# A layer's windowed attention: one overlaid score square per head in place of two, and a 0/1 band multiplied in after the turn

## The chip, the cores and the metric

One core of one Trainium2 chip runs the whole program. The metric is device time in microseconds of one execution, median of several. The engines named here are TensorE (PE), VectorE (DVE), ScalarE (ACT) and GpSimd (POOL). They run their own instruction streams in order and meet only at semaphores.

## The reference

The program is a first block (short convolution, sparse attention, cross attention, FFN) and then a second block of two layers, on 512 tokens of width 1024. The change is in the second block's attention, which has 16 query heads of width 64, two key/value heads and a window of 128 tokens:

```
def sliding_window_attention(q, k, v, sinks):          # BLOCK = WINDOW_2 = 128
    qb = q.reshape(B, nb, BLOCK, N_KV_HEADS, GROUP, HEAD_DIM)
    kb, vb = band(k), band(v)              # previous block of 128 keys, then the query's own block
    s = einsum('bnqkgd,bnskd->bnkgqs', qb, kb) * HEAD_DIM ** -0.5
    rel = qi + BLOCK - sj                  # qi: 0..127, sj: 0..255
    mask = (rel >= 0) & (rel < WINDOW_2) & (kpos >= 0)
    s = where(mask, s, -inf)
    m = maximum(max(s), sink)
    p = exp(s - m);  p = p / (sum(p) + exp(sink - m))
    o = einsum('bnkgqs,bnskd->bnqkgd', p, vb)
```

With window and block both 128, query r of a block sees key s of its own block where s <= r, and key s of the previous block where s > r. So of the two 128 x 128 squares of a head each position is live in exactly one. Around the attention stand a wide input projection, a 31-tap convolution with a layer norm, gates, an output projection and an FFN.

## The kernel before

Everything is float32. The large products are made of three float32r products each (hi*hi, hi*lo, lo*hi; lines 415 to 417), fed by weight units that DMA brings, ACT splits into hi (line 297) and DVE into lo (line 301, in halves lines 793 and 797). They are nearly all of PE's work.

The attention of a layer is 32 jobs (`LJ`). Job j is one pair of heads (e = 0, 1) and one block of 128 queries; `block_of` takes blocks 1, 2, 3 and last block 0, so jobs 0 to 23 have two squares (previous block and own block) and jobs 24 to 31 only their own. The jobs run through a software pipeline, written out by hand: a loop over steps t, of which each engine has its own version, in the same order of t. Of a job j:

- PE, step j, `scores`: two products of 64 x 256 columns into two PSUM banks (`score_bank`, alternating between two pairs).
- DVE, step j, `softmax`: for each e one fused instruction (line 2415) that scales the scores, adds the mask, writes `lprob` and takes the running minimum of the negated scores, over 256 columns; after these, the reciprocal of the row sums of job j-1 (line 2419).
- ACT, step j, `exps` (line 2260): two exponentials of 257 columns (the 257th is the sink, put there by POOL, `sink_column`), with row sums.
- POOL, step j+1, `scaled` (line 2590): multiplies the 2 x 256 probabilities of a row with the reciprocal.
- PE, step j+3 (`LAG_T`), `turn` (line 2120): four transposes of 128 x 128 into bank 4.
- ACT, step j+3, `copy_turned` (line 2267): bank 4, 512 columns, to `lprobT` (two buffers). It is the first thing ACT does in a step.
- PE, step j+4 (`LAG_V`), `values` (line 2133): four products with the values into bank 6, last thing in a step but for the sums below.
- DVE, step j+4, `gated` (line 2427): bank 6 times the gate into `sga`.

In the jobs of block 0 all of it is half as wide, and `turn` and `values` have two instructions for each four.

Between `turn` and `values` PE does a number of the layer's large products, `FILL_AT`[t]; steps 0, 4, 8, 11 and 13 have none. At the end of step 3 PE sums the convolution's output over channels (`ln_sum`, line 2170), which waits for the last of 124 convolution taps on DVE (line 2345; three taps ahead of the loop, three in step 0, two in step 1). DVE takes the mean (line 2473) and subtracts it (line 2476), ACT squares (line 2289; channels 0, 1 in step 3, 2, 3 in step 4), POOL adds the squares (line 2604; one addition in step 6, two in step 7), and PE sums them at the end of step 7 (line 333).

The tail: from step 29 POOL adds the convolution's half to the attention's half of output tile k = t-29 (`merged`, line 2595), ACT rounds it (`merged_hi`, line 2273, last in ACT's step), DVE takes the remainder (`merged_lo`, line 2440, from step 30), and PE multiplies tile k with the output weights in step 32+k, k = 0 to 3 (`OUT_AT`: nine products in a step); tiles 4 to 7 come after the loop. Tile 7 is added on DVE in the last step, ahead of that step's `merged_lo`.

Of the kernel before, what the change touches and what calls it, by code (L numbers as in the profile page):

```python
# [25 lines left out]
I32 = mybir.dt.int32  # L26
ALU = mybir.AluOpType
# [73 lines left out]
def build(nc, w, x, mem, pos, pack, tables, cmask, w2, wg, rope2, out):  # L101
    ctx = ExitStack()
    with ctx:
# [118 lines left out]
        tab2 = place("tab2", [P, 2 * T + 2 * P], F32, a)  # L222
        cos2, sin2 = tab2[:, 0:T], tab2[:, T:2 * T]
        perm2, heads2 = tab2[:, 2 * T:2 * T + P], tab2[:, 2 * T + P:]
# [6 lines left out]
        lprob = place("lprob", [P, 4, 2, 2 * P + 2], F32, b)  # L231
        lprobT = place("lprobT", [P, 2, 4, P], F32, b)
# [411 lines left out]
        def _(sp):  # L644
# [38 lines left out]
        kc_step, vc_done, kc_rope, kcm_ready, kcm_dup, vblk_ready = (  # L683
            sem(n) for n in ("kc_step", "vc_done", "kc_rope", "kcm_ready", "kcm_dup", "vblk_ready"))
# [115 lines left out]
        def mixer1_pe(pe):  # L800
# [122 lines left out]
            def c_scores(i):  # L923
                if i == 0:
                    pe.wait_ge(kcm_dup, 1)
# [150 lines left out]
        def mixer1_act(act):  # L1076
# [100 lines left out]
            act.wait_ge(kcm_ready, 1)  # L1177
            act.activation(kcm[HD:P, :, :], kcm[0:HD, :, :], ACT.Copy).then_inc(kcm_dup, 1)
# [105 lines left out]
        def mixer1_dve(dve):  # L1284
# [104 lines left out]
            dve.tensor_copy(kcm[0:HD, :, 0:NCMP], kc2[:, :, :]).then_inc(kcm_ready, 1)  # L1389
# [456 lines left out]
        def cross_dve(dve):  # L1846
# [76 lines left out]
            for j in range(11):  # L1923
# [5 lines left out]
        l_u, l_ugs, l_sig, l_a, l_tap, l_q, l_vt, l_v_turned, l_v = (sem("l_" + n) for n in (  # L1929
            "u", "ug_scaled", "sigmoid", "a", "tap", "q", "v_raw", "v_turned", "v"))  # L1930
# [7 lines left out]
        A = {n: sem("a_" + n) for n in ("scores", "max", "exp", "rec", "scaled", "turned", "turned_copied",  # L1938
                                        "pv", "gated")}
# [9 lines left out]
        LAG_T, LAG_V = 3, 4  # L1949
# [16 lines left out]
        MERGE_HI_AT, MERGE_LO_AT = 29, 30  # L1966
        OUT_AT = {32: (0,), 33: (1,), 34: (2,), 35: (3,)}
        STEPS = LJ + LAG_V

        def prob_at(j):  # L1970

            return (0, 1, 3, 2)[j % 4]
# [25 lines left out]
        def layer_pe(pe, L):  # L1998
# [38 lines left out]
            for n in range(3, V_FILL):  # L2037
# [8 lines left out]
                if n == V_KV + 1:  # L2046
                    pe.wait_ge(l_vt, L + 1)
                    for b_ in range(QB):
                        mm = pe.transpose(bank[:, AUX, b_ * P:(b_ + 1) * P], acc[:, b_ * P:(b_ + 1) * P], ident[:, :])
                    mm.then_inc(l_v_turned, 1)  # L2050
# [62 lines left out]
            def turn(j):  # L2113
                first = 1 if block_of(j) == 0 else 0
# [32 lines left out]
            for t in range(STEPS):  # L2147
# [11 lines left out]
                if t in OUT_AT:  # L2159
                    if t == LJ:  # L2160
# [26 lines left out]
        def layer_act(act, L):  # L2187
# [21 lines left out]
            for n in range(V_FILL):  # L2209
# [6 lines left out]
                if n == V_KV:  # L2216
                    act.wait_ge(unit_done, u.n + 1)

                    act.activation(acc[:, :], bank[:, 2 * u.slot + 1, :], ACT.Copy).then_inc(l_vt, 1)
# [17 lines left out]
                if n == V_KV + 1:  # L2237
                    act.wait_ge(l_v_turned, L + 1)
# [15 lines left out]
            def exps(j):  # L2254
                c0 = P if block_of(j) == 0 else 0
                act.wait_ge(sink_in, L * LJ + j + 1)
                for e in range(2):
                    act.wait_ge(A["max"], (L * LJ + j) * 2 + e + 1)
                    row = lprob[:, prob_at(j), e, c0:2 * P + 1]
                    act.activation(row, row, ACT.Exp, bias=asm(j, 0, e), scale=-1.0, accum_out=asm(j, 4, e)).then_inc(A["exp"], 1)  # L2260

            def copy_turned(j):
                act.wait_ge(A["turned"], L * LJ + j + 1)
                if j >= 2:
                    act.wait_ge(A["pv"], L * LJ + j - 1)
                first = 1 if block_of(j) == 0 else 0
                act.activation(lprobT[:, j % 2, :, :].rearrange("p (e c) t -> p e c t", e=2)[:, :, first:, :],
                               bank[:, 4, :].rearrange("p (e c t) -> p e c t", e=2, c=2)[:, :, first:, :], ACT.Copy)\
# [55 lines left out]
        def layer_dve(dve, L):  # L2324
# [76 lines left out]
            def softmax(j, o):  # L2401

                j, o = j if j < LJ else None, o if 0 <= o < LJ else None
                if j is not None:
                    c0 = P if block_of(j) == 0 else 0
                    if j == 0:
                        dve.wait_ge(q_inv, L * 2 + 2)
                    if j in (2, 3):
                        dve.wait_ge(q_rope, L * 9 + j + 6)
                    if j >= 4:  # L2410
                        dve.wait_ge(A["turned"], L * LJ + j - 3)
                    for e in range(2):
                        c = 2 * (j % 8) + e
                        dve.wait_ge(A["scores"], (L * LJ + j) * 2 + e + 1)
                        dve.tensor_tensor_reduce(lprob[:, prob_at(j), e, c0:2 * P], bank[:, score_bank(j) + e, c0:2 * P], mask_b[:, c0:2 * P],  # L2415
                                                 query_factor(j, e), neg_sink[:, L, c:c + 1], ALU.add, ALU.min, asm(j, 0, e)).then_inc(A["max"], 1)
                if o is not None:
                    dve.wait_ge(A["exp"], (L * LJ + o + 1) * 2)
                    dve.reciprocal(asm(o, 12), asm(o, 4)).then_inc(A["rec"], 1)  # L2419

# [127 lines left out]
        def _(pool):  # L2548
# [28 lines left out]
            def sink_column(L, j):  # L2577
                if j in (2, 3):
                    pool.wait_ge(q_rope, L * 9 + j + 6)
# [3 lines left out]
                pool.tensor_copy(lprob[:, prob_at(j), :, 2 * P], sinks).then_inc(sink_in, 1)  # L2583

            def scaled(L, j):
                c0 = P if block_of(j) == 0 else 0
# [172 lines left out]
```

## Time and profile before

| | |
|---|---|
| time, median of 3 runs | 2248.24 us (2246.92 to 2248.31) |
| span of the profiled execution | 2246.4 us (the page gives no other time for it) |
| busy in it | PE 2224.9, PE weight loads 1821.7, DVE 1245.1, ACT 885.6, POOL 280.7 us |
| chain that ended last | PE 93%, DVE 3%, POOL 1%, ACT 1%, issue 1% |
| granted PE clock | 0.999 mean |
| the loop over the steps in the two layers | 1033 to about 1155 and 1725 to about 1847 us from the span's start |

Times in a timeline are microseconds from the span's start. PE's instructions overlap: the time that one costs is the distance from its start to the next one's start, not its duration. A duration on DVE, ACT and POOL also overlaps the next one of that engine by some tens of nanoseconds. A bracket at a line's end is the engine's idle time ahead of it and what ended it.

### The profile page before, as it was taken

What the parts mean: (1) busy time and instruction counts of PE and PEld (TensorE: products, weight loads), DVE (VectorE), ACT (ScalarE), POOL (GpSimd) and SP (SyncE); (2) the same over time, 40 slices, a digit from 0 to 9 for tenths busy, and PEclk for the clock granted to TensorE, in tenths of its full rate; (3) what the DMA queues carried; (4) which work ended last, traced back from release to release, by engine and by line L of the source; (5) the groups of instructions that cost most, each with busy time, mean ns of one, the idle gap of its engine ahead of it and who ended that gap; (6) DMA issues with size and microseconds to landing.
All of it is one profiled execution on the core that took longest, in us unless ns stands there. A gap on an engine that the chain in (4) does not pass through costs nothing.

```text
span 2246.4 us, 29245 instructions
## 1 busy us (share of the span) xinstructions
PE 2224.9 (99%) x11388; PEld 1821.7 (81%) x11388; DVE 1245.1 (55%) x1836; ACT 885.6 (39%) x1363; POOL 280.7 (12%) x273
## 2 busy tenths in 40 slices
PE   9999999999999999999999999999999999999999
PEld 7877888898888888886778888888887668888887
DVE  6467656445444225999664444333889664544422
ACT  5545454354333225234744333222323753433321
POOL 3000032011000001014331000001003442000000
PEclk9999999999999999999999999999999999999999
DMA  6221033122222231321122222222221112322222
GB/s 223 100 76 57 20 121 126 55 72 99 103 102 93 94 113 69 113 75 57 56 77 81 107 93 93 100 106 105 104 84 57 39 66 85 113 102 104 94 101 86
DMA packets 30484, 203.19 MB, mean 90 GB/s; under 512 B 3504, under 2 KB 4144, under 8 KB 6704
## 3 DMA queue, kind: packets, MB, share of 16 engines
q1 hardware_dynamic: 29088, 197.34, 24.4%
q10 hardware_dynamic: 1296, 4.46, 0.5%
q8 instruction: 69, 1.13, 0.2%
q14 instruction: 31, 0.25, 0.0%
HBM read 199.69 MB, written 2.10 MB: 90 GB/s over the span
## 4 chain that ended last, share of the span: by engine, by line
PE 93%; DVE 3%; POOL 1%; ACT 1%; issue 1%; DMA 0%; ACTq 0%; DVEq 0%; POOLq 0%
PE bank L415 26%; PE bank L417 26%; PE bank L416 26%; PE bank L2110 1%; PE bank L1002 1%; PE bank L2120 1%; PE bank L2133 1%; PE bank L973 1%; PE bank L2028 1%; POOL acc L324 1%; PE bank L990 1%; PE bank L2010 1%; PE bank L1593 1%; PE bank L1570 1%; PE bank L515 1%
## 5 line engine op out<-in xcount | busy, mean ns | idle before, releaser
L415 PE MATMUL bank<-x_hi,w_hi 128*128 128x512 f32 (+1 forms) x2032 | 789.9, 389 | 5.9 <-DVE x_lo L1766 2.3
L417 PE MATMUL bank<-x_hi,w_lo 128*128 128x512 f32 (+1 forms) x2032 | 775.0, 381 | 0.0
L416 PE MATMUL bank<-x_lo,w_hi 128*128 128x512 f32 (+1 forms) x2032 | 774.1, 381 | 0.0
L301 DVE TENSOR_TENSOR w_lo<-w_raw,w_hi 128x2048 fp32r<-128x2048 f32 x167 | 386.2, 2313 | 412.3 <-ACT w_hi L297 412.3
L297 ACT ACTIVATE w_hi<-w_raw 128x2048 fp32r<-128x2048 f32 x167 | 319.7, 1916 | 585.8 <-PE bank L417 583.9
L415 PEld LDWEIGHTS bank<-x_hi,w_hi 128*128 128x128 f32 x2032 | 382.1, 188 | 83.6 <-issue 6.8
L417 PEld LDWEIGHTS bank<-x_hi,w_lo 128*128 128x128 f32 x2032 | 381.9, 188 | 74.9
L416 PEld LDWEIGHTS bank<-x_lo,w_hi 128*128 128x128 f32 x2032 | 382.4, 188 | 72.7 <-issue 2.9
L415 PE MATMUL bank<-f_hi,w_hi 128*128 128x512 f32 (+1 forms) x572 | 213.3, 373 | 0.0
L416 PE MATMUL bank<-f_lo,w_hi 128*128 128x512 f32 (+1 forms) x572 | 213.2, 373 | 0.0
L417 PE MATMUL bank<-f_hi,w_lo 128*128 128x512 f32 (+1 forms) x572 | 213.2, 373 | 0.0
L2345 DVE SCALAR_TENSOR_TENSOR cy<-la,gains,cy 128x512 f32<-128x512 f32 x240 | 173.9, 794 | 0.0
L563 DVE TENSOR_TENSOR bank<-bank,rbc 128x512 f32<-128x512 f32 x66 | 46.0, 697 | 167.6 <-PE bank L417 159.6
L415 PEld LDWEIGHTS bank<-f_hi,w_hi 128*128 128x128 f32 x572 | 107.7, 188 | 19.0
L416 PEld LDWEIGHTS bank<-f_lo,w_hi 128*128 128x128 f32 x572 | 107.7, 188 | 18.9
L417 PEld LDWEIGHTS bank<-f_hi,w_lo 128*128 128x128 f32 x572 | 107.7, 188 | 18.7
L324 POOL TENSOR_TENSOR acc<-acc,sq 128x512 f32<-128x512 f32 (+1 forms) x48 | 77.6, 1618 | 144.2 <-ACT sq L308 140.4
L552 ACT ACTIVATE f_hi<-bank 128x512 f32 x66 | 39.6, 599 | 115.5 <-DVE bank L569 115.5
L571 DVE TENSOR_TENSOR f_lo<-bank,f_hi 128x512 f32 x66 | 45.7, 692 | 58.4 <-ACT f_hi L552 58.4
L2590 POOL TENSOR_TENSOR lprob<-lprob,small 128x512 f32<-128x512 f32 (+1 forms) x64 | 61.9, 967 | 123.6 <-DVE small L2419 77.8
L2260 ACT ACTIVATE lprob<-lprob,small 128x257 f32<-128x257 f32 (+1 forms) x128 | 60.5, 475 | 31.5 <-DVE small L2415 30.9
L324 POOL TENSOR_TENSOR acc<-sq 128x512 f32<-128x512 f32 (+1 forms) x8 | 14.4, 1801 | 442.8 <-ACT sq L308 442.8
(355 smaller groups left out, 2637.2 us busy)
## 6 DMA issues: line engine op xcount, KB each, us to landing
w_raw<-w_d SPq DMA_DIRECT2D x184, 1024.0 KB, 4.8
out_d<-h SPq DMA_DIRECT2D x8, 256.0 KB, 6.6
h<-x_d ACTq DMA_DIRECT2D x3, 512.0 KB, 9.2
tab<-rope_d ACTq DMA_DIRECT2D x2, 640.0 KB, 3.9
memT<-mem_d ACTq DMA_DIRECT2D x1, 1024.0 KB, 4.8
w_raw<-w_d SPq DMA_DIRECT2D x2, 256.0 KB, 4.1
h<-x_d ACTq DMA_DIRECT2D x2, 256.0 KB, 5.8
w_raw<-w_d SPq DMA_DIRECT2D x1, 512.0 KB, 6.6
```

Source lines behind the costliest of these rows:

```text
L297: act.activation(w_hi[:, u.slot, :], w_raw[:, u.slot, :], ACT.Copy).then_inc(hi_ready, 1)
L301: dve.tensor_tensor(w_lo[:, u.slot, :], w_raw[:, u.slot, :], w_hi[:, u.slot, :], ALU.subtract).then_inc(lo_ready, 1)
L324: pool.tensor_tensor(acc[:, 0:width], sq[:, 0, 0:width] if k == 1 else acc[:, 0:width], sq[:, k % 2, 0:width], ALU.add).then_inc(acc_ready, 1)
L415: pe.matmul(dst, wh[:, k, cols], hi[:, kx_, at:at + width], start=start, stop=False)
L416: pe.matmul(dst, wh[:, k, cols], lo[:, kx_, at:at + width], start=False, stop=False)
L417: return pe.matmul(dst, wl[:, k, cols], hi[:, kx_, at:at + width], start=False, stop=stop)
L552: act.activation(pick(f_hi, j, i), up, ACT.Copy).then_inc(f_hi_done, 1)
L563: dve.tensor_tensor(g, g, rbc[:, :], ALU.mult).then_inc(gu_scaled, 1)
L571: dve.tensor_tensor(pick(f_lo, j, i), up, pick(f_hi, j, i), ALU.subtract).then_inc(f_lo_done, 1)
L2260: act.activation(row, row, ACT.Exp, bias=asm(j, 0, e), scale=-1.0, accum_out=asm(j, 4, e)).then_inc(A["exp"], 1)
L2345: dve.scalar_tensor_tensor(out=cy[:, m, :], in0=src, scalar=wt, in1=cy[:, m, :], op0=ALU.mult, op1=ALU.add).then_inc(l_tap, 1)
L2590: pool.tensor_tensor(row, row, asm(j, 12).unsqueeze(2).to_broadcast([P, 2, 2 * P - c0]), ALU.mult).then_inc(A["scaled"], 1)
```

## The change

- Jobs 0 to 23: DVE first copies, with one predicated copy for both heads, the previous block's square over the own block's square wherever s > r. The own square then holds the 128 live scores of a row. The predicate is the own square's mask (bf16, read as 16-bit integers; nonzero where s > r). `max`, `exp`, `scaled` and `turn` then handle one square per head: 128 columns, and two transposes per job.
- DVE's order in a step is now predicated copy(t), reciprocal(t-1), then the two fused instructions of t. The copy waits for both heads' scores, the fused instructions for the copy.
- `copy_turned` moves 256 columns, and waits for POOL's `banded` of two jobs before.
- New on POOL: `banded`, in step j+3 after `scaled`: one multiplication of 512 columns (256 in block 0) that makes from the turned square two squares, times the 0/1 bands r > s and r <= s. It waits for `copy_turned`(j) and for `values`(j-2). The result `lband` goes to `values`, whose four products stay.
- `LAG_V` is 5, `STEPS` 37. `merged`, `merged_hi`, `merged_lo` and the output products all start one step later (30, 30, 31, 33). `FILL_AT` and the other tables stay, so step 32 has no large product.
- The table read by DMA per layer grows by 256 columns. `lprob`, `lprobT` are smaller and start elsewhere, so waits on the rope move from jobs 2, 3 to job 0. Some semaphores are joined.

```
@@ LAG_T, LAG_V = 3, 4      ->  LAG_T, LAG_V = 3, 5
@@ MERGE_HI_AT, MERGE_LO_AT = 29, 30  ->  30, 31
@@ OUT_AT = {32: (0,), 33: (1,), 34: (2,), 35: (3,)}  ->  {33: (0,), 34: (1,), 35: (2,), 36: (3,)}
 turn(j):
-                for e in range(2):
-                    for c in range(first, 2):
-                        mm = pe.transpose(bank[:, 4, (2 * e + c) * P:(2 * e + c + 1) * P], lprob[:, prob_at(j), e, c * P:(c + 1) * P], ident[:, :])
+                for e in range(2):
+                    mm = pe.transpose(bank[:, 4, e * P:(e + 1) * P], lprob[:, prob_at(j), e, 0:P], ident[:, :])
 values(j):
-                pe.wait_ge(A["turned_copied"], L * LJ + j + 1)
+                pe.wait_ge(A["banded"], L * LJ + j + 1)
...
-                                       lprobT[:, j % 2, 2 * e + c, :], start=(c == first), stop=(c == 1))
+                                       lband[:, j % 2, c, e, :], start=(c == first), stop=(c == 1))
 copy_turned(j):
                 if j >= 2:
-                    act.wait_ge(A["pv"], L * LJ + j - 1)
+                    act.wait_ge(A["banded"], L * LJ + j - 1)
...
+                act.activation(lprobT[:, j % 2, :, :].rearrange("p e t -> p (e t)"), bank[:, 4, 0:2 * P], ACT.Copy)\
 softmax(j, o):
+                first = j is not None and block_of(j) == 0
+                if j is not None and not first:
+                    pair = bank[:, score_bank(j):score_bank(j) + 2, :]
+                    dve.wait_ge(A["scores"], (L * LJ + j + 1) * 2)
+                    dve.copy_predicated(pair[:, :, P:2 * P], mask_b[:, P:2 * P].bitcast(U16).unsqueeze(1).to_broadcast([P, 2, P]),
+                                        pair[:, :, 0:P]).then_inc(A["packed"], 1)
                 if o is not None:
                     dve.wait_ge(A["exp"], (L * LJ + o + 1) * 2)
                     dve.reciprocal(asm(o, 12), asm(o, 4)).then_inc(A["rec"], 1)
+                if j is not None:
...
+                    if not first:
+                        dve.wait_ge(A["packed"], L * 24 + j + 1)
+                    for e in range(2):
...
+                        dve.tensor_tensor_reduce(lprob[:, prob_at(j), e, 0:P], bank[:, score_bank(j) + e, P:2 * P],
+                                                 mask_b[:, P:2 * P] if first else mask_b[:, 0:P],
+                                                 query_factor(j, e), neg_sink[:, L, c:c + 1], ALU.add, ALU.min, asm(j, 0, e)).then_inc(A["max"], 1)
 scaled(L, j):
-                pool.tensor_tensor(row, row, asm(j, 12).unsqueeze(2).to_broadcast([P, 2, 2 * P - c0]), ALU.mult).then_inc(A["scaled"], 1)
+                pool.tensor_tensor(row, row, asm(j, 12).unsqueeze(2).to_broadcast([P, 2, P]), ALU.mult).then_inc(A["scaled"], 1)
+            def banded(L, j):
+                first = 1 if block_of(j) == 0 else 0
+                shape = [P, 2 - first, 2, P]
+                pool.wait_ge(A["turned_copied"], L * LJ + j + 1)
+                if j == 0:
+                    pool.wait_ge(q_rope, L * 9 + 9)
+                if j >= 2:
+                    pool.wait_ge(A["pv"], L * LJ + j - 1)
+                pool.tensor_tensor(lband[:, j % 2, first:, :, :], lprobT[:, j % 2, :, :].unsqueeze(1).to_broadcast(shape),
+                                   band2[:, first:, :].unsqueeze(2).to_broadcast(shape), ALU.mult).then_inc(A["banded"], 1)
 POOL's loop:
+                for t in range(STEPS):
...
+                    if t < LJ:
+                        sink_column(L, t)
+                    if t in (6, 7):
+                        sums_of_squares(L, (0,) if t == 6 else (1, 2))
+                    if 0 <= t - 1 < LJ:
+                        scaled(L, t - 1)
+                    if 0 <= t - LAG_T < LJ:
+                        banded(L, t - LAG_T)
+                    if MERGE_HI_AT <= t:
+                        merged(L, t - MERGE_HI_AT)
```

## Rows read from the trace of the kernel before

**Rows 1.** The page, part 4: the chain of work that ended last.

```profile
PE 93%; DVE 3%; POOL 1%; ACT 1%; issue 1%; DMA 0%; ACTq 0%; DVEq 0%; POOLq 0%
```

**Rows 2.** Line 2120 (turn) asked for: PE idle before it, us, times, both layers.

```profile
  ACT lprobT L2267: 4.4, 4
```

**Rows 3.** Timeline of PE, steps 24 and 27: start, us, instruction.

```profile
1120.93 0.66 PE L2120 MATMUL bank<-ident,lprob 128*128 128x128 f32 x4
1121.34 0.47 PE L415 MATMUL bank<-c_hi,w_hi 128*128 128x512 f32 x1
...
1122.90 0.66 PE L2133 MATMUL bank<-lprobT,lv 128*64 128x128 f32 x8
1123.49 0.37 PE L2110 MATMUL bank<-lq 64*128 64x128 f32 x1
...
1129.20 0.44 PE L2120 MATMUL bank<-ident,lprob 128*128 128x128 f32 x2
1129.39 0.48 PE L415 MATMUL bank<-c_hi,w_hi 128*128 128x512 f32 x1
```

**Rows 4.** Groups of instructions by shape, DVE: count, busy us, mean ns, idle before.

```profile
L2415 DVE CUSTOM_DVE_ANT_0 lprob<-bank,mask_b,neg_sink 128x256 f32<-128x256 f32 x96 | 48.2, 539 | 5.9 <-PE bank L2110 5.8
...
L2427 DVE SCALAR_TENSOR_TENSOR sga<-sga,bank 128x128 f32<-128x128 f32 x64 | 18.4, 287 | 64.9 <-PE bank L2133 64.9
...
L2377 DVE TENSOR_TENSOR bank<-bank,rbc 128x512 f32<-128x512 f32 x20 | 12.9, 686 | 3.0 <-PE bank L417 3.0
...
L2415 DVE CUSTOM_DVE_ANT_0 lprob<-bank,mask_b,neg_sink 128x128 f32<-128x128 f32 x32 | 11.8, 408 | 0.9 <-PE bank L2110 0.9
```

**Rows 5.** The same view, POOL.

```profile
L2590 POOL TENSOR_TENSOR lprob<-lprob,small 128x512 f32<-128x512 f32 x48 | 52.1, 1085 | 98.3 <-DVE small L2419 52.6 <-ACT lprob L2260 45.6
...
L2590 POOL TENSOR_TENSOR lprob<-lprob,small 128x256 f32<-128x256 f32 x16 | 9.8, 615 | 25.2 <-DVE small L2419 25.2
```

**Rows 6.** The same view, ACT.

```profile
L2267 ACT ACTIVATE lprobT<-bank 128x512 f32<-128x512 f32 x48 | 28.4, 591 | 29.3 <-PE bank L2120 29.0
...
L2267 ACT ACTIVATE lprobT<-bank 128x256 f32<-128x256 f32 x16 | 6.0, 376 | 4.3 <-PE bank L2120 4.3
```

**Rows 7.** Windows, the loop's first 12 us: busy us of PE, PEld, DVE, ACT, POOL.

```profile
1033.00:1045.00 12.00, 11.85 (x53) 7.77 (x54) 11.93 (x28) 3.27 (x14) 4.05 (x6) 1.00 0.00 0
```

**Rows 8.** Timeline of DVE, steps 1 and 3: the last taps; the mean.

```profile
1041.53 1.90 DVE L2345 SCALAR_TENSOR_TENSOR cy<-la,gains,cy 128x512 f32<-128x512 f32 x2
...
1047.22 0.69 DVE L2473 TENSOR_SCALAR acc<-bank 128x512 f32<-128x512 f32 x1 [0.34 <-PE bank L2170]
```

**Rows 9.** Timeline of PE, steps 3 to 7.

```profile
1043.48 3.70 PE L2170 MATMUL bank<-cy,ones 128*128 128x512 f32 x8
...
1050.53 0.63 PE L2120 MATMUL bank<-ident,lprob 128*128 128x128 f32 x4 [0.91 <-ACT lprobT L2267]
...
1059.00 0.48 PE L2110 MATMUL bank<-lkx,lq 64*128 64x256 f32 x1
...
1062.52 1.05 PE L333 MATMUL bank<-ones,la 128*128 128x1 f32 x8 [0.26 <-POOL la L2604]
```

**Rows 10.** Timeline of POOL, step 7.

```profile
1059.16 3.31 POOL L2604 TENSOR_TENSOR la<-la 128x512 f32<-128x512 f32 x2
```

**Rows 11.** Timeline of DVE: line 793 beside rows 10, and alone.

```profile
1059.32 2.01 DVE L793 TENSOR_TENSOR w_lo<-w_raw,w_hi 128x1024 fp32r<-128x1024 f32 x1
...
1100.89 1.22 DVE L793 TENSOR_TENSOR w_lo<-w_raw,w_hi 128x1024 fp32r<-128x1024 f32 x1
```

**Rows 12.** Timeline of POOL, steps 29 and 30.

```profile
1136.55 1.27 POOL L2595 TENSOR_TENSOR sgb<-sgb,sga 128x512 f32<-128x512 f32 x1
...
1140.93 1.76 POOL L2595 TENSOR_TENSOR sgb<-sgb,sga 128x512 f32<-128x512 f32 x1
```

**Rows 13.** Timeline of PE, step 32.

```profile
1143.77 0.41 PE L2120 MATMUL bank<-ident,lprob 128*128 128x128 f32 x2 [1.29 <-ACT lprobT L2267]
```

**Rows 14.** Timeline of ACT, step 30.

```profile
1142.72 0.63 ACT L2273 ACTIVATE o_hi<-sgb 128x512 fp32r<-128x512 f32 x1 [1.95 <-POOL sgb L2595]
```

More of the change, by code:

```diff
@@ L26 @@
 I32 = mybir.dt.int32
+U16 = mybir.dt.uint16
 ALU = mybir.AluOpType
@@ L230, in build @@
         b = [a[0]]
-        lprob = place("lprob", [P, 4, 2, 2 * P + 2], F32, b)
-        lprobT = place("lprobT", [P, 2, 4, P], F32, b)
+        lprob = place("lprob", [P, 4, 2, P + 1], F32, b)
+        lprobT = place("lprobT", [P, 2, 2, P], F32, b)
+        lband = place("lband", [P, 2, 2, 2, P], F32, b)
         bank = ctx.enter_context(nc.psum_tensor("bank", [P, 8, T], F32))
@@ L1937, in build @@
         co_done, co_ready, mg_sum, mg_hi, mg_lo = (sem("l_" + n) for n in ("co_done", "co_ready", "mg_sum", "mg_hi", "mg_lo"))
-        A = {n: sem("a_" + n) for n in ("scores", "max", "exp", "rec", "scaled", "turned", "turned_copied",
-                                        "pv", "gated")}
+        A = {n: sem("a_" + n) for n in ("scores", "packed", "max", "exp", "rec", "scaled", "turned", "turned_copied",
+                                        "banded", "pv", "gated")}
         sink_in = sem("a_sink_in")
@@ L2263, in copy_turned @@
                 act.wait_ge(A["turned"], L * LJ + j + 1)
+                if j == 0:
+                    act.wait_ge(q_rope, L * 9 + 9)
                 if j >= 2:
-                    act.wait_ge(A["pv"], L * LJ + j - 1)
-                first = 1 if block_of(j) == 0 else 0
-                act.activation(lprobT[:, j % 2, :, :].rearrange("p (e c) t -> p e c t", e=2)[:, :, first:, :],
-                               bank[:, 4, :].rearrange("p (e c t) -> p e c t", e=2, c=2)[:, :, first:, :], ACT.Copy)\
+                    act.wait_ge(A["banded"], L * LJ + j - 1)
+                act.activation(lprobT[:, j % 2, :, :].rearrange("p e t -> p (e t)"), bank[:, 4, 0:2 * P], ACT.Copy)\
                    .then_inc(A["turned_copied"], 1)
@@ L2419, in softmax @@
                     dve.reciprocal(asm(o, 12), asm(o, 4)).then_inc(A["rec"], 1)
+                if j is not None:
+                    if j == 0:
+                        dve.wait_ge(q_inv, L * 2 + 2)
+                    if j >= 4:
+                        dve.wait_ge(A["turned"], L * LJ + j - 3)
+                    if not first:
+                        dve.wait_ge(A["packed"], L * 24 + j + 1)
+                    for e in range(2):
+                        c = 2 * (j % 8) + e
+                        if first:
+                            dve.wait_ge(A["scores"], (L * LJ + j) * 2 + e + 1)
+                        dve.tensor_tensor_reduce(lprob[:, prob_at(j), e, 0:P], bank[:, score_bank(j) + e, P:2 * P],
+                                                 mask_b[:, P:2 * P] if first else mask_b[:, 0:P],
+                                                 query_factor(j, e), neg_sink[:, L, c:c + 1], ALU.add, ALU.min, asm(j, 0, e)).then_inc(A["max"], 1)
             def gated(j):
@@ L2617, in _ @@
                     pool.tensor_tensor(lcos[:, t % 2, 0:T], lq[:, rope_at(t), :], cos_q[:, :] if t else cos2, ALU.mult).then_inc(q_cos, 1)
-                for j in range(LJ + 1):
-                    if j == 0:
+                for t in range(STEPS):
+                    if t == 0:
                         pool.wait_ge(setup_step, SINKS_NEGATED)
                         pool.wait_ge(q_ss, L * 9 + 9)
-                    if j < LJ:
-                        sink_column(L, j)
-                    if j in (6, 7):
-                        sums_of_squares(L, (0,) if j == 6 else (1, 2))
-                    if j > 0:
-                        scaled(L, j - 1)
-                    if j > 28:
-                        merged(L, j - 29)
-                for k in range(LJ - 28, DT - 1):
-                    merged(L, k)
+                    if t < LJ:
[8 more added lines that the diff above has]
+                        merged(L, t - MERGE_HI_AT)
                 for n in (1, 2) if L + 1 < LAYERS else (1,):
@@ L2729 @@
     r, s = np.arange(P)[:, None], np.arange(P)[None, :]
-    masks = [np.where(s > r, 0, NEG), np.where(s <= r, 0, NEG)]
+    masks = [np.zeros((P, P)), np.where(s <= r, 0, NEG)]
     for b in range(QB):
```

65 lines of the change are left out of this document (25 added, 40 removed).

## The prediction, made before the changed kernel ran

> **What bounds the kernel now.** I read the chain that ended last first: 93% of it is PE [rows 1], and the table above has PE busy for 99% of the span. So the time is PE's own work plus whatever makes PE wait, and nothing saved on another engine counts by itself. The waits come next. In both layers' loops together `turn` waited 4.4 us in 4 waits for `copy_turned` [rows 2]; two of them are to be seen in layer one, 0.91 us in step 5 [rows 9] and 1.29 us in step 32 [rows 13], and twice their sum is the 4.4. Beside them PE waited 0.26 us for POOL's squares in step 7 [rows 9]. Everywhere else in the loop DVE, ACT and POOL are ahead. The question is therefore: how much shorter is PE, and do these three waits grow?
>
> **PE's saving.** Four transposes take 1120.93 to 1121.34, 0.41 us; two take 1129.20 to 1129.39, 0.19 us [rows 3]. 0.22 us less for each of 24 jobs in 2 layers is 10.56 us. Scores, values and large products keep their number. Values are moved one step later, which alone costs nothing; only where PE waits anyway does it matter that they no longer stand ahead of the wait.
>
> **DVE's step.** Removed: twice 539 - 408 ns, 0.26 us [rows 4]. Added: a predicated copy of 128 x 256 in PSUM. The trace has none. From below it is a 128 x 128 operation on PSUM, 287 ns, from above a 128 x 512 one, 686 ns [rows 4]; on the line between them 256 columns take 0.42 us, which I take, and 0.07 us since the next instruction must wait for its end. A step of DVE gets 0.23 us longer (0.03 to 0.5). From step 8 to step 28 DVE has room for this.
>
> **The front, steps 0 to 7.** DVE has no room here: it is busy 11.93 of the first 12 us [rows 7].
> - The convolution's last taps begin at 1041.53 and last 1.90 us [rows 8], and PE's channel sums start on their heels at 1043.48 [rows 9]. Two longer DVE steps move them to 1043.9, so the first saved transposes are lost.
> - DVE takes the mean at 1047.22 after 0.34 us idle [rows 8]. Four longer steps (0.92) less that slack make 1047.8. Centring, ACT's squares and then `copy_turned`(1) follow; the copy is shorter by 0.59 - 0.38 us [rows 6]. So `turn`(2), at 1050.53 before [rows 9], starts at 1050.9, although PE, without the values ahead of it, is there 1 us earlier than before.
> - Step 7: `banded`(3) is queued on POOL ahead of the two additions of squares, and it waits for `values`(1), the last work of PE's step 6. That step ended at 1059.00 (the next scores, rows 9) and will end at 1058.9 (0.4 later, two turns shorter). `banded` is of the shape 128 x 512, 1.09 us [rows 5], the sink column 0.2, two additions at 1.09 each are 2.2: 1062.4. In the trace the two took 3.31 us [rows 10], 1.1 more, beside DVE's line 793, which took 2.01 instead of 1.22 us [rows 11]. With that clash it is 1063.5; I take 1063.0 for sums that started at 1062.52 [rows 9].
> - Loss of the front: 0.5 us later, the 5 turns saved by then (1.1), and one group of values (1122.90 to 1123.49, 0.59 us, rows 3) still to be done: 2.2 us a layer. With the copy at 0.29 and no clash it is 1.2, with 0.69 and the clash 3.3.
>
> This clash is where the Trainium skill bears on the case. What the rows show is that both engines lengthen, POOL by 1.1 and DVE by 0.8 us [rows 10, 11]. The page "SBUF — State Buffer", section "SBUF: two separate sides", says that DVE with two SBUF inputs and GpSimd reading SBUF take one pair of ports in turns, the loser waiting for the whole instruction; the trace agrees with 0.8 and 1.1 us for instructions of about that length. By that rule 24 more POOL instructions a layer, set off by the same event as DVE's gating, meet the line 793/797 splits again and again; that is the second rival below.
>
> **The middle, steps 8 to 28.** No wait of PE for these engines stands in the trace, so 19 turns' saving is real. I allow 0.3 us a layer for one clash that reaches PE in part, 0 to 1.0.
>
> **The tail, steps 29 to 36.** Before, POOL's `merged` takes 1.27 to 1.76 us [rows 12], ACT waits 1.95 us for it and rounds in 0.63 [rows 14], and only then does its next step copy the turned square, for which PE waits 1.29 us [rows 13]. Now `banded` closes a ring: `merged`(k) on POOL, `merged_hi`(k) on ACT, `copy_turned`(28+k) behind it, `banded`(28+k) on POOL, which stands ahead of `merged`(k+1). One round is 1.27 to 1.76, 0.63, 0.38 [rows 6] and 0.62 [rows 5]: 2.9 to 3.4 us; I take 3.1.
> - `turn`(29) in step 32 waits for the first round. It begins when `values`(25) ends step 30, with `banded`(27): 0.1 + 0.6 + 1.5 + 0.6 + 0.4 = 3.2 us, while PE has step 31 to do, some 1.7 us. A wait of 1.5 to 1.6 in place of 1.29: 0.3 more.
> - `turn`(30) waits for the next round, 3.1 us later. PE has in step 32 only two transposes, 0.19, and four value products, half of 0.59 and a little for the change, together 0.6, since the output products now start in step 33: a new wait of 2.5 us.
> - `turn`(31): step 33 has nine products, 2.25 us at the pace of six in 1121.34 to 1122.90 [rows 3], and 0.55 for turn and values. The ring is slower by 0.3 to 0.5.
> - Tile 5's remainder on DVE stands behind tile 7's addition, which needs all of POOL's `merged`; 0 to 0.6, in the bound only.
> The loss is 3.3 us a layer, from 2.0 (quick `merged`) to 4.5.
>
> **At nothing:** ACT's shorter exponentials, the 128 KB more of table (loaded long before use, beside products), the joined semaphores, the moved rope waits.
>
> **Sum.** Per layer -5.28 + 2.2 + 0.3 + 3.3 = +0.5, for both +1.0 us: the profiled execution's span goes from 2246.4 to 2247.4. The median of runs lies 1.84 us above that span, which I keep: 2248.24 + 1.0, about 2249.3. All low bounds give 3.2 a layer, 2 x (3.2 - 5.28) = -4.2, 2244.1; all high ones 8.8, +7.0, 2255.3.
>
> **Rivals.**
> - *The waits do not grow together* (0.25). For it: PE waits only 4.4 us in the loops [rows 2], and most of the chain steps are a guess in their overlap. If nothing is given back it is 2248.24 - 10.56 = 2237.7; if only the front or only the tail is, some 2.5 us a layer, 2248.24 - 10.56 + 5 = 2242.7. Against it: step 32 is left without products, which is plain from the code.
> - *Port clashes make DVE late as well* (0.17): slower. `banded` starts when `values` ends, and so does DVE's gating with a split half right behind it. Each meeting costs DVE 0.8 us [rows 11]. It decides if the meetings fall where PE already waits for what DVE does next, in steps 5, 6 and 29 of each layer: 3 x 0.8 x 2 = 4.8 over the forecast, 2254.1.
> - *The predicated copy is far dearer than 0.69 us* (0.08): slower. Each 0.3 us more goes four times through the full front: 1.2 a layer, 2.4 in all, and 0.9 us more makes 2256.5. For it only that no row has one.
> - *The transposes are not the price*, two of them costing as much as four in front of a product: against it stand rows 3. It would be 2248.24 + 11.5 = 2259.7; I give it no chance of its own.
>
> **How the numbers follow.** The forecast has 0.50; alone it spans 2244.1 to 2252.7. A measurement of this kernel tells 0.2%, 4.5 us, from no change: faster is below 2243.7, slower above 2252.7. Faster: most of the first rival, 0.22. Slower: the second and third and the forecast's upper end, 0.23. Same: 0.55. The range goes from 2242.5, which takes in the half-way case of the first rival, to 2255.3.
>
> **What would show it.** Right: `turn` with two transposes and 0.19 us; PE's wait in step 5 grown to about 2 us, in step 7 to 1.5, and a new one near 2.5 us at `turn` in step 33, all of them ending with POOL or ACT; DVE's predicated copy near 0.42 us. Wrong: no new wait in step 33 (then the ring does not bind and the time falls by 5 us or more), or waits spread over steps 8 to 28 (then it is the clashes, or the copy).

## The result and the profile after

The changed kernel takes 2265.16 us (median, 2263.2 to 2265.8) against 2248.19 for the kernel before on the same chip: ratio 1.0073, 95% interval 1.0062 to 1.0085. It is 17 us slower, where 2249.3 was forecast and 2255.3 was the range's end. Its profiled execution spans 2261.5 us (before 2246.4), with a mean granted clock of 0.995 (before 0.999). The four executions are 2.1 us (two) and 3.3 us (two) longer than their spans, those of the kernel before 1.8 to 2.1.

The chain of the kernel after [rows 1 for before]: PE's share has fallen and DVE and POOL have gained.

```profile
PE 89%; DVE 5%; POOL 2%; issue 2%; ACT 1%; DMA 0%; ACTq 0%; DVEq 0%; POOLq 0%
```

PE's waits over 0.15 us in layer one's loop, after: engine and line, what it waited for, us in total, times, longest.

```profile
PE bank L2121 <- ACT lprobT L2268: 5.8, 4, 2.4
PE bank L336 <- POOL la L2621: 2.3, 1, 2.3
PE bank L418 <- DVE o_lo L2448: 2.0, 2, 1.4
PE bank L2113 <- issue: 0.7, 1, 0.7
PE bank L418 <- issue: 0.3, 1, 0.3
PE bank L2134 <- DVE sga L2435: 0.2, 1, 0.2
```

Before, `turn` waited 4.4 us in both layers [rows 2]; now it waits 5.8 in one, the column sums 2.3 (0.26 in rows 9), and the output products 2.0 (before nothing). Where they stand, in PE's timeline after; these rows answer to [rows 9, 13]:

```profile
1050.28 0.41 PE L2121 MATMUL bank<-ident,lprob 128*128 128x128 f32 x2 [1.69 <-ACT lprobT L2268]
...
1063.99 1.05 PE L336 MATMUL bank<-ones,la 128*128 128x1 f32 x8 [2.27 <-POOL la L2621]
...
1143.74 0.41 PE L2121 MATMUL bank<-ident,lprob 128*128 128x128 f32 x2 [1.34 <-ACT lprobT L2268]
1146.93 0.66 PE L2121 MATMUL bank<-ident,lprob 128*128 128x128 f32 x2 [2.42 <-ACT lprobT L2268]
1147.25 0.78 PE L418 MATMUL bank<-o_hi,w_hi 128*128 128x512 f32 x1
1147.82 0.63 PE L419 MATMUL bank<-o_lo,w_hi 128*128 128x512 f32 x1
1148.25 0.63 PE L420 MATMUL bank<-o_hi,w_lo 128*128 128x512 f32 x1
...
1151.37 0.70 PE L2134 MATMUL bank<-lband,lv 128*64 128x128 f32 x4
...
1160.74 0.50 PE L418 MATMUL bank<-o_hi,w_hi 128*128 128x512 f32 x1 [0.55 <-DVE o_lo L2448]
...
1164.50 0.50 PE L418 MATMUL bank<-o_hi,w_hi 128*128 128x512 f32 x1 [1.43 <-DVE o_lo L2448]
```

The rows behind 1146.93 show what the forecast had no term for. Products follow each other every 0.43 us, not every 0.23 [rows 3]: the nine from 1147.25 to 1151.37 take 4.12 us, where nine at full clock take 2.25. The windows (busy us of PE, PEld, DVE, ACT, POOL; then the granted clock) say the same, in both layers' front and tail:

```profile
1064.00:1068.00 4.00, 4.00 (x29) 2.67 (x29) 1.78 (x8) 1.83 (x3) 3.47 (x5) 0.85 0.00 0
1068.00:1072.00 4.00, 4.00 (x21) 2.89 (x21) 1.06 (x7) 3.49 (x12) 0.97 (x3) 0.72 0.01 2
...
1146.00:1150.00 4.00, 3.07 (x9) 2.52 (x10) 0.69 (x1) 1.70 (x5) 2.62 (x3) 0.50 0.01 2
1150.00:1154.00 4.00, 4.00 (x18) 2.62 (x17) 1.40 (x2) 0.94 (x1) 1.78 (x2) 0.73 0.00 0
...
1766.00:1770.00 4.00, 4.00 (x20) 2.70 (x17) 2.26 (x12) 3.63 (x8) 2.58 (x4) 0.57 0.00 0
1845.00:1852.00 7.00, 5.30 (x18) 3.67 (x18) 0.82 (x2) 2.75 (x5) 3.40 (x5) 0.51 0.00 0
```

0.50 is the lower level, 1.2 GHz; I call such a piece of time a stretch at half clock. The tail's stretch begins inside the 2.42 us wait, which follows a wait of 1.34 (read by single microseconds, the clock is 0.65 from 1145 and 0.50 from 1146, and the wait ends at 1146.93). The front's begins just before 1067, 2 us behind the column sums, and these stand behind the 2.27 us wait. In the kernel before, no microsecond of the loops is below 1.00. The front's first stretch costs 4 x 0.15 + 4 x 0.28 = 1.7 us, the tail's 4.12 - 2.25 = 1.9 us on those nine products and some 0.4 on the turn and the values beside them: by my estimate about 2 us each, 7 to 8 us in all.

The price of the new instructions was close to the forecast. Groups by shape, after (count, busy us, mean ns, idle before):

```profile
L2606 POOL TENSOR_TENSOR lband<-lprobT,tab 128x512 f32<-128x512 f32 x48 | 63.8, 1329 | 26.2 <-PE bank L2134 25.7
...
L2425 DVE CUSTOM_DVE_ANT_0 lprob<-bank,mask_b,neg_sink 128x128 f32<-128x128 f32 x128 | 47.5, 408 | 3.4 <-DVE bank L2409 0.2
...
L2409 DVE COPY_PREDICATED bank<-mask_b,bank 128x256 f32<-128x256 uint16 x48 | 20.2, 420 | 7.0 <-PE bank L2113 7.0
L2606 POOL TENSOR_TENSOR lband<-lprobT,tab 128x256 f32<-128x256 f32 x16 | 13.2, 823 | 15.7 <-PE bank L2134 12.2 <-ACT lprobT L2268 3.5
...
L2494 DVE TENSOR_TENSOR c_lo<-cy,c_hi 128x512 fp32r<-128x512 f32 x8 | 8.1, 1049 | 0.0
```

The predicated copy is 0.42 us, as taken. `banded` is 1.33 and 0.82 us, not 1.09 and 0.62 [rows 5]. DVE's `c_lo` has grown from 700 ns in the kernel before to 1049: POOL's `banded` now runs beside it.

### The profile page after: what moved, and what is told of

It reads as the page before. It is cut to its first block, busy times and chain, and to the rows that moved or that the text cites. A ratio compares the mean times of both kernels' runs of the same rounds, so it can differ in the third digit from the quotient of the medians.

```text
span 2261.5 us, 29225 instructions
## 1 busy us (share of the span) xinstructions
PE 2224.1 (98%) x11292; PEld 1816.3 (80%) x11292; DVE 1261.0 (56%) x1884; ACT 866.5 (38%) x1363; POOL 341.1 (15%) x337
## 4 chain that ended last, share of the span: by engine, by line
PE 89%; DVE 5%; POOL 2%; issue 2%; ACT 1%; DMA 0%; ACTq 0%; DVEq 0%; POOLq 0%
PE bank L418 26%; PE bank L420 25%; PE bank L419 25%; DVE cy L2345 1%; PE bank L1005 1%; PE bank L2134 1%; PE bank L2113 1%; PE bank L2121 1%; PE bank L976 1%; POOL acc L327 1%; PE bank L993 1%; PE bank L2013 1%; PE bank L1596 1%; PE bank L1573 1%; POOL sgb L2612 1%
## 5 line engine op out<-in xcount | busy, mean ns | idle before, releaser
L2606 POOL TENSOR_TENSOR lband<-lprobT,tab 128x512 f32<-128x512 f32 (+1 forms) x64 | 77.0, 1203 | 41.9 <-PE bank L2134 37.9
L2260 ACT ACTIVATE lprob<-lprob,small 128x129 f32<-128x129 f32 x128 | 50.5, 396 | 68.4 <-DVE small L2425 60.4
```

Of the source, the lines that this page charges most:

```text
L2606: pool.tensor_tensor(lband[:, j % 2, first:, :, :], lprobT[:, j % 2, :, :].unsqueeze(1).to_broadcast(shape), band2[:, first:, :].unsqueeze ...
```

## How the runs are compared

Beside the median I give the length of a layer: from its first scores to the next layer's first scores in the profiled execution. It leaves out the stages ahead, whose end varies from 1031.4 to 1034.6 us in these profiles; some of them, the kernel before among them, have a stretch at half clock there too (222 to 228 us in the kernel before, 224 to 231 in the first experiment). A layer's length belongs to one execution, the time is the median of several, and the two need not move by the same amount. Before: 1033.16 to 1725.28, 692.1 us. After: 1032.98 to 1732.75, 699.8 us, 7.7 more. The ledger of layer one, step against step: 5.3 us of transposes saved; lost 0.8 in step 5, 0.3 in step 6, 2.0 in step 7, about 2 by the clock behind it, 0.6 where `c_lo` is late in step 18, 0.1 and 2.4 at the turns of steps 32 and 33, about 2 by the clock there, 0.4 by values that now come last, 0.5 and 1.5 at output tiles 4 and 5: 12.6 to 13 us.

## Experiments

All are the changed kernel with the edit shown, unless it is said otherwise; `...` marks lines left out.

**Fill two gaps.** `spare` issues 128 x 256 products into a part of a bank that nobody reads, behind the waits that this bank needs.

```
+ if t == 33: spare(16, 5)              # ahead of turn(30)
  ...
  if t == AT_SS:
+     spare(14, 7)                      # ahead of the column sums
      pe.wait_ge(ln_add, L * 3 + 3)
```

> The changed kernel with unused products put where PE waits: 14 products of 128x256 float32r at the end of step 7, ahead of the wait for the squares, and 16 at the start of step 33, ahead of turn(30). They go to a free PSUM bank and nothing reads them. In the changed kernel's trace PE runs at the lower of its two clocks twice in each layer, from about 1066.6 to 1070.2 us after the 2.27 us wait of step 7 and from about 1146.9 to 1151.5 us after the 2.42 us wait of step 33. Theory (the waits themselves cost, and on top of them the clock that they bring down, some 2 us each of four times): the granted clock stays at the upper level in both places, the waits are filled, and the time falls by about 8 us, from 2265.2 to 2257. Rival (the clock falls for another reason, for instance the mix of small products, or the spare products delay the work behind them): clock record and time as in the changed kernel, 2265 or above.

Measured 2257.76 us, 1.0041 [1.0026, 1.0055]; layer 697.7. The tail's stretches are gone and so is the second layer's front one; the first layer's stays:

```profile
1068.00:1072.00 4.00, 4.00 (x19) 3.03 (x18) 1.23 (x6) 3.84 (x12) 1.32 (x3) 0.67 0.01 2
...
1146.00:1150.00 4.00, 3.65 (x23) 2.72 (x22) 0.69 (x1) 1.42 (x3) 3.01 (x4) 1.00 0.01 2
```

With work added, and three of the four stretches gone, the kernel is 7.4 us faster (5.6 us in the profiled spans); the waits were filled, not removed. That is the clock's part, shown.

**No band for block 0**, where it changes nothing: there the diagonal mask is in the scores already, and the masked probabilities are zero.

```
-                lband[:, j % 2, c, e, :]
+                lprobT[:, j % 2, e, :] if first else lband[:, j % 2, c, e, :]
...
-    if 0 <= t - LAG_T < LJ:   banded(L, t - LAG_T)
+    if 0 <= t - LAG_T < 24:   banded(L, t - LAG_T)
```

The waits go with it: in block 0 `values` waits for `copy_turned`, and `copy_turned` for `values` of two jobs before.

> The changed kernel without the band multiplication for the 8 jobs of block 0, whose mask already makes the future keys zero: their values read the turned square as ACT copied it, the same result. The step order is the same. Theory (the ring merged - merged_hi - copy_turned - banded on POOL and ACT sets the tail): the wait at turn(30) falls from 2.42 to about 1.2 us, the clock does not drop there, and the waits for tiles 4 and 5 (0.55 and 1.43 us) nearly go: 5 to 6 us a layer, 2265.2 to about 2254. Rival (the tail is lost to step 32 having no large product, whatever POOL does): the wait at turn(30) stays above 2 us and the time falls by less than 4 us.

Measured 2254.89, 1.0033 [1.0019, 1.0047]; layer 692.9. The turns of the tail wait 0.64, 0.99 and 0.64 us (and twice 0.21 ahead of them), tile 4 waits 0.21, tile 5 nothing, and the tail has full clock. So `banded` is what closed the ring and what made tiles 4 and 5 late. The front's 2.3 us wait is the same in both layers, yet only the second has a stretch at half clock (1758 to 1765). This one begins inside the wait, ahead of the column sums, which start at 1758.46.

**The squares' additions all in step 6**, ahead of `banded`(3).

```
- if t in (6, 7):
-     sums_of_squares(L, (0,) if t == 6 else (1, 2))
+ if t == 6:
+     sums_of_squares(L, (0, 1, 2))
```

> The changed kernel with one part of POOL's order changed: all three additions of squares stand in step 6, ahead of scaled(5) and banded(3), instead of one in step 6 and two in step 7 behind banded(3). Theory (banded(3), which waits for values(1) at the end of PE's step 6 and takes 2.34 us there, pushes the additions out): PE's 2.27 us wait in step 7 shrinks below 0.5 us, the lower clock after it goes with it, 3.5 to 4 us a layer, 2265.2 to about 2257.5. Rival (POOL simply has more work than the front has room for, and whatever is put behind is late): the wait reappears at turn or values of steps 8 and 9, and the time falls by 3 us at most.

Measured 2257.7, 1.0042 [1.0026, 1.0059]; layer 696.8. The 2.27 us wait is gone, three quarters of it come back at the turns of steps 9 and 10 (1.50 and 0.22 us), and both front stretches are gone; the tail's stay, at waits of 1.34 and 2.41. So the wait moved, as the rival said, and the time fell by 7.5 us, as the theory said. Not all of that is the front's: the tail's stretches are shorter here at the same waits (1145 to 1149 and 1841 to 1845, for 1145 to 1152 and 1845 to 1852), and no run tells why.

**Two groups of products moved from steps 29 and 30 to step 32.**

```
- FILL_AT = {... 29: 3, 30: 3, 31: 1}
+ FILL_AT = {... 29: 2, 30: 2, 31: 1, 32: 2}
```

> The changed kernel with two of the large product groups of steps 29 and 30 moved to step 32, which had none. The work is the same. Theory that the empty step 32 makes the loss of the tail: the 2.42 us wait at turn(30) falls to about 1.0, the clock does not drop after it, 3.6 us a layer, 2265.2 to about 2258. Theory that the ring of POOL and ACT sets the tail: with less PE work ahead of step 32 the wait at turn(29) grows from 1.34 by what turn(30) loses, the later waits for tiles 4 and 5 stay, and only the clock can be won: 2261 to 2265.

Measured 2258.36, 1.0040 [1.0027, 1.0053]; layer 696.5. The three turns wait 1.39, 1.06 and 0.54 us; none is long, and the tail has full clock. The turns' waits fell by 0.8 us a layer in sum, the layer by 3.3. The time is the first theory's. But tile 5 still waits 1.42 us and tile 4 0.35, as the second theory said, and in the first experiment they wait 1.40 and 0.35, both with full clock in the tail: so the tiles' waits are POOL's and DVE's, and the half clock adds only some 0.2 us to tile 4's.

**Fill the wait of step 5 too.**

```
+ if t == 5: spare(12, 6)               # with the two of the first experiment
```

> The changed kernel with unused products ahead of the column sums in step 7 and in step 33, as once before, and 12 more in step 5 where TensorE waits 1.69 us for the turned square. Theory (every idle of TensorE in the front stretch bears on its clock): the stretch at half clock after step 8 that stayed in the first layer is gone too, 2256 us against 2257.8 with two gaps filled. Rival (the wait in step 5 is too far ahead of the fall to matter; the column sums themselves, eight products of one column, are what leaves the array idle): the stretch stays, 2257.8 us.

Measured 2257.2, 1.0037 [1.0024, 1.0050]; layer 697.7. PE's waits between steps 4 and 9 are 0.32 and 0.43 us and the first layer's stretch stands where it was, 1067 to 1071. The stretch stayed, as the rival said. The second layer has none, so the sums alone do not decide it either.

**And products between the column sums**, as well as the three fillings:

```
  for b_ in range(QB):
+     spare product
      mm = matmul(bank[:, 7, b_:b_ + 1], squares[..], ones[:, 0:1])
+     if b_ < QB - 1: spare product
```

These are 15 products, two between each pair of sums and one ahead, not the seven of the expectation.

> The changed kernel with unused products in the waits of steps 5, 7 and 33, and now seven more between the eight one-column products of the column sums. Theory (the column sums, 1.05 us in which the array does almost nothing, are what brings the clock down after step 8): no stretch at half clock in either layer, 2 us less for the one that goes and some 1.6 us more for the added products: about 2257. Rival (neither these idles nor the sums decide it): the stretch at 1067 to 1071 stays, about 2259.

Measured 2257.97, 1.0042 [1.0027, 1.0057]; layer 696.7. Full clock in both layers:

```profile
1064.00:1068.00 4.00, 3.57 (x33) 2.76 (x31) 0.76 (x3) 0.91 (x3) 2.64 (x5) 1.00 0.01 2
1068.00:1072.00 4.00, 4.00 (x29) 2.78 (x27) 2.24 (x13) 3.76 (x8) 2.40 (x4) 1.00 0.01 2
```

So with products of 256 columns among the column sums the clock stays at 1.00, and without them, the waits filled alike, it fell to 0.50 in the first layer. Whether it is what stands between the sums that counts, or only that there is more work near by, the run does not tell: it is one profiled execution, and the same products were not tried in another place.

**Everything 1.7 us later**: 12 unused products ahead of the first scores, in the changed kernel and in the kernel before.

> The changed kernel with 12 unused products (some 1.7 us) ahead of the first scores of each layer, all the attention the same but later. Theory (the waits alone decide where the clock falls): four stretches at half clock as before the edit, 2268.5 us. Rival (it depends also on when a wait comes, as the front's stretch that was missing in one layer of three of the kernels suggests): at least one of the four goes or moves by more than the shift, 2264 to 2267.

> The kernel before with the same 12 products ahead of the first scores. Theory (its waits of 0.9, 0.3, 1.3 and 0.9 us are too short whenever they come): full clock throughout, 2251.5 us. Rival (it was only lucky in when its waits came): a stretch at half clock in one of the layers, 2253 to 2255.

Measured 2265.69, 1.0075 [1.0057, 1.0094], with four stretches, at 1069, 1147, 1768 and 1850; and 2251.54, 1.0013 [1.0003, 1.0023], with none. So the shift removed no stretch from the changed kernel and brought none into the kernel before, whose waits are 1.3 us at most. Two limits: the first time is only 0.5 us above the changed kernel's where 3.3 was expected (step 5 waits 1.50 us for 1.69, and the last stretch is 1850 to 1855 for 1845 to 1852), and the profiled execution of the second was the fastest of eight (2249.81, clock 1.000); six others, 2251.07 to 2252.79, have 0.998 or 0.999, and no trace shows where they lost it. The moment does count: with equal waits the clock fell in one layer and not in the other in three of the experiments above.

**Turn twice**: PE makes the second pair of transposes again, into an unused half of the bank.

```
+ for c in range(1 if block_of(j) == 0 else 0, 2):
+     mm = pe.transpose(bank[:, 4, (e + 2 - 2 * c) * P:...], lprob[:, prob_at(j), e, 0:P], ident)
```

> The changed kernel, but TensorE turns each overlaid square twice (the second copy goes to an unused part of the bank): for blocks 1 to 3 it does as many transposes as the kernel before. Theory: TensorE bounds the loop outside its four waits, so the transposes are worth 0.22 us each job in some 20 of 24 jobs a layer: 8 to 10 us slower than the changed kernel, 2274 us. Rival (the saved transposes bring nothing, since the end is set by other engines): within 2 us of 2265.

Measured 2271.42, 1.0102 [1.0087, 1.0118]; layer 704.2, 4.4 more than the changed kernel. With the waits of steps 5 and 7, shorter by 0.22 and 0.39, that is 5.0 us for 24 jobs, against the 5.28 of the forecast. This is rough: the front's stretch at half clock is longer here, 1064 to 1071, and the tail's shorter, 1153 to 1156, and the median rose by 6.3 us where 8 to 10 were expected (8.4 in the profiled spans). The saving is real.

**Both edits together** (no band for block 0, early squares).

> The changed kernel with two of the earlier edits together: no band for block 0 (the turned square is used as it is), and the three additions of squares all in step 6. Theory (waits of TensorE and the stretches at half clock that follow them make up the whole loss): the two edits gave 10.3 and 7.5 us alone; both took the half-clock stretch of one layer's front, about 2 us, so together 15.8 us, 2249.4 us; reckoned from the kernel before it is 5.28 saved per layer less 2.5 (front waits), 0.4 (tail), 0.55 (c_lo behind a band) and 0.4, so 1.5 us better per layer, 2245.4 us. Expected 2247, between 2245 and 2250, no stretch at half clock inside the attention stage. Rival (the changed kernel is slow for another reason that the waits only accompany, such as VectorE being late all along the loop): no better than 2253.

Measured 2250.05, 1.0010 [1.0001, 1.0019]; layer 692.6. One stretch remains, in the second layer at 1742 to 1746, where none was expected. It comes with the wait of step 5, and the same wait in the first layer (1.69 us as well) left the clock at 1.00:

```profile
1742.09 0.66 PE L2121 MATMUL bank<-ident,lprob 128*128 128x128 f32 x2 [1.69 <-ACT lprobT L2273]
```

The two edits take 15 of the 17 us away, but the reckoning from the kernel before (2245.4) was too good.

**And for block 0 the values four steps behind again**, on top of both edits.

```
- STEPS = LJ + LAG_V
+ STEPS = LJ + 4
+ def values_at(t):
+     return [j for j in range(LJ) if t == j + (5 if block_of(j) else 4)]
...
- MERGE_HI_AT, MERGE_LO_AT = 30, 31
- OUT_AT = {33: (0,), 34: (1,), 35: (2,), 36: (3,)}
+ MERGE_HI_AT, MERGE_LO_AT = 29, 30
+ OUT_AT = {32: (0,), 33: (1,), 34: (2,), 35: (3,)}
```

> As the kernel with both edits, and for block 0 the values follow four steps behind the scores instead of five (two heads' values in step 28), the merging and the output tiles one step earlier, as in the kernel before. Theory: what the fifth step costs is the products of step 32 that no longer lie beside the tail's ring and values shifted past them, 0.2 to 0.4 us per layer: 0.4 to 1 us below the kernel with both edits. Rival: the step is what made TensorE wait in the tail, and 2 us per layer go, 4 us in all.

Measured 2245.71, 0.9988 [0.9979, 0.9997]; layer 690.4: the best version, 2.5 us faster than the kernel before and 4.3 faster than the last one, as the rival said. The profiled execution has full clock throughout, but it is the fastest of eleven (2243.02 to 2247.91 us, clocks 1.000 to 0.998), so the eight below 1.000 hold stretches at half clock that no trace shows. PE's waits in the tails of the two, first without the edit, then with it:

```profile
1140.63 0.41 PE L2121 MATMUL bank<-ident,lprob 128*128 128x128 f32 x2 [0.64 <-ACT lprobT L2273]
1140.96 0.44 PE L2137 MATMUL bank<-lprobT,lv 128*64 128x128 f32 x4
1142.40 0.41 PE L2121 MATMUL bank<-ident,lprob 128*128 128x128 f32 x2 [0.99 <-ACT lprobT L2273]
...
1145.89 0.41 PE L2121 MATMUL bank<-ident,lprob 128*128 128x128 f32 x2 [0.64 <-ACT lprobT L2273]
...
1156.55 0.50 PE L418 MATMUL bank<-o_hi,w_hi 128*128 128x512 f32 x1 [0.22 <-DVE o_lo L2453]
```

```profile
1139.39 0.41 PE L2125 MATMUL bank<-ident,lprob 128*128 128x128 f32 x2
1140.48 0.47 PE L418 MATMUL bank<-o_hi,w_hi 128*128 128x512 f32 x1 [0.68 <-DVE sgb L2454]
```

With the fifth step, step 32 has no products between two turns (1140.63, 1142.40). Without it the output products lie there, and all of the tail's waits are one of 0.68 us, less than the 1.29 before [rows 13]. With it they are 2.9 with the two small ones of 0.21 ahead.

**The kernel before with early squares only.**

> The kernel before with the three additions of squares all in step 6 and nothing else. It tells whether the best version owes its time to the change or to this edit. Theory: TensorE waits only 0.26 us for these additions in the kernel before, so at most 0.5 us in both layers: 2247.7 to 2248.4. Rival (the edit is worth as much there as in the changed kernel, where it gave 7.5 us): 2244 or less.

Measured 2248.40, 1.0000 [0.9991, 1.0009]; layer 692.5. In the kernel before this edit gives nothing, so the best version's gain over it is not the edit's alone.

## Why the prediction was wrong

- *PE's saving, 0.22 us for 24 jobs a layer*: right (two transposes 0.19 us, turning twice 5.0 a layer).
- *DVE's step, +0.23 us*: right, 0.42 us for the copy.
- *The front, steps 0 to 7, "2.2 us a layer"*: mechanism right, size short. The mean was not late at all (1046.98, forecast 1047.8): the last two taps took 1.41 us in place of 1.90 [rows 8], and the channel sums began at 1043.25. The wait of step 5 was 1.69 for about 2. But in step 7 the wait was 2.27 for 1.5, the sums 1.0 us behind the forecast's 1063.0. About half of that is the clash, which the forecast had taken at half its size and which fell on `banded` and not on the additions; the other half is dearer instructions, `banded` at 1.27 alone and the two additions at 2.50, for 1.09 and 2.2. POOL's timeline after, then DVE's:

```profile
1058.44 0.61 POOL L2595 TENSOR_TENSOR lprob<-lprob,small 128x256 f32<-128x256 f32 x1
1059.01 2.34 POOL L2606 TENSOR_TENSOR lband<-lprobT,tab 128x512 f32<-128x512 f32 x1
1061.30 0.18 POOL L2589 COPY lprob<-neg_sink 128x2 f32<-128x2 f32 x1
1061.44 2.50 POOL L2621 TENSOR_TENSOR la<-la 128x512 f32<-128x512 f32 x2
```

```profile
1058.98 1.22 DVE L796 TENSOR_TENSOR w_lo<-w_raw,w_hi 128x1024 fp32r<-128x1024 f32 x1
```

DVE's split began 0.03 us ahead of `banded`, kept its 1.22 us, and `banded` took 2.34, 1.07 more than the 1.27 us it takes alone: the whole chain to the sums is later by it. The upper end of the forecast put the sums at 1063.5; they came at 1063.99. (The Trainium skill, "SBUF — State Buffer", section "SBUF: two separate sides", says that the one that comes first holds the shared ports and the other blocks for all of that instruction; by that rule the extra would be about 1.2 us, an estimate from the split's length, and the trace agrees with 1.07.) Loss of steps 5 to 7: 3.1 us.
- *The middle, 0.3 us*: 0.6, from one such clash, `c_lo` in step 18. It is the second rival's kind. That rival counted 24 new POOL instructions a layer; there are 32, and they met DVE's more than once (a split in step 5 took 2.35 us for 1.22 before, the other two `c_lo` 1.74 for 1.28). But in step 5 DVE's next instruction, the centring, no longer met POOL and took 1.28 for 2.13, so that DVE was only 0.3 us later there, which is PE's new wait of 0.30 in step 6; in the middle only this pair of `c_lo` reached PE. DVE's timeline after (the split, then `c_lo`; two `c_lo` took 1.35 us before):

```profile
1050.35 2.35 DVE L796 TENSOR_TENSOR w_lo<-w_raw,w_hi 128x1024 fp32r<-128x1024 f32 x1
...
1097.07 2.30 DVE L2494 TENSOR_TENSOR c_lo<-cy,c_hi 128x512 fp32r<-128x512 f32 x2
```

- *The tail, "3.3 us a layer"*: the ring is as told. `turn`(29) waits 1.34 for 1.5 to 1.6, `turn`(30) 2.42 for 2.5. What was left "in the bound only" was a real wait: tiles 4 and 5 cost 0.5 and 1.5 us. POOL's timeline after:

```profile
1146.87 0.96 POOL L2606 TENSOR_TENSOR lband<-lprobT,tab 128x256 f32<-128x256 f32 x1 [0.44 <-ACT lprobT L2268]
1147.79 1.27 POOL L2612 TENSOR_TENSOR sgb<-sgb,sga 128x512 f32<-128x512 f32 x1
1152.22 0.74 POOL L2606 TENSOR_TENSOR lband<-lprobT,tab 128x256 f32<-128x256 f32 x1 [3.16 <-PE bank L2134]
...
1156.61 5.23 POOL L2612 TENSOR_TENSOR sgb<-sgb,sga 128x512 f32<-128x512 f32 x3
```

POOL idles 3.16 us for PE's values, made later by the half clock, and then has three `merged` left, 1.74 us each beside DVE's splits, with the tiles behind them. Tile 5's wait stays at 1.4 us with full clock in the tail (first and fourth experiment), so it is not the clock's.
- *The step that failed is the sum itself*: it added waits and priced PE's work at full clock throughout. The waits it forecast (about 2, 1.5, 1.5, 2.5 us) were near those that came (1.69, 2.27, 1.34, 2.42), and four stretches at half clock came with them, 7 to 8 of the 16 us between forecast and result. Of the rest some 4 us are tiles 4 and 5 in two layers, 2 us the front, 0.6 us `c_lo`, less 0.8 by which the turns of the tail lost less than forecast. Nearly 2 us lie outside the span: from forecast to profile the spans differ by 14.1 (2247.4 to 2261.5), and the median lies 3.7 above that span, not the 1.84 that was kept. About 1 us stays open.

Settled by runs: the clock's part in sum (filling the gaps, products in step 32), the ring and the tiles (no band for block 0), the queue of step 7 (early squares), the fifth step (four behind again). Not settled: why one layer and not the other kept full clock at equal waits; why a stretch lasts 3.4 us in one place and 6.6 in another; and in the best version the waits are 2.0 us a layer more than before while the transposes give 5.3, of which 1.7 arrive: `c_lo` has some 0.6 of the difference, and 1.0 I don't find in any wait over 0.15 us. Some 0.2 of it is step 3, where the saved transposes are lost as forecast: from `turn`(0) to `turn`(1) the profile has 5.46 us, before 5.47, since the channel sums start only behind DVE's last tap.

## What to carry to other kernels

A wait of the bounding engine has to be priced twice: its length, and the granted clock behind it. Look for places where two waits, or a wait and a run of small products like the column sums, stand close together; moving existing products there (step 32) costs nothing and gave 6.8 us here, more than the 0.8 us a layer by which the turns' waits shrank. The second price is not certain: at equal waits it came in one layer and not in the other. When an added instruction joins a ring between engines at a loop's end, where there is no other work, look first whether it is needed there at all: for block 0, whose masked entries are zero already, it was not, and dropping it gave 10.3 us of the 17, and with the squares moved ahead and the step undone that it had asked for, the loss became 2.5 us of gain.

## What was not expected of the hardware

- Waits of 1.34 and 2.42 us, 0.8 us of work apart, were enough for the half clock (0.50 from 1146 to 1152); waits of 1.39, 1.06 and 0.54 in the same place came without it. A single wait of 1.69 us stood with a fall in one layer (both edits, 1742), and the same wait in the other layer without.
- With the waits of steps 5 and 7 filled the clock still fell to 0.50, 2 us behind eight one-column products that the profile shows as 1.05 us of busy PE; with larger products among them it did not. In another run it fell ahead of them (1758).
- An elementwise product on POOL with both inputs broadcast took 1.33 us for 512 elements and 0.82 for 256, beside 1.09 and 0.62 with one [rows 5]; part of it is contention (beside nothing it took 1.26 to 1.31, and 0.73).
